# GpSimd takes the tables of the state-space branch, with new task tables for both first layers

## The reference

```python
lam_bar = jnp.exp(lam * dt)
b_bar = ((lam_bar - 1.0) / lam)[..., None] * b_c
bu = jnp.einsum("blgh,gph->blgp", uf.astype(jnp.complex64), b_bar)
_, states = lax.associative_scan(combine, (a_elems, bu), axis=1)
y = jnp.einsum("blgp,ghp->blgh", states, c_c).real
```

## Time and profile before

| what | value |
|---|---|
| median of three runs | 2157.72 us |
| the profiled execution | 2156.08 us, span 2154.3 us |
| TensorE busy | 2131.7 us, 99% of the span |
| VectorE busy | 1640.0 us, 76% |
| ScalarE busy | 1212.4 us, 56% |
| GpSimd busy | 56.4 us, 3% |
| granted TensorE clock | 0.999 of full speed |

### The profile page before, as it was taken

One profiled execution on the slowest core, in us unless ns is written; L12 is line 12 of the kernel. 1 busy time (PEld: TensorE's weight loads), 2 busy tenths in 40 slices (PEclk: granted clock), 3 DMA queues, 4 the chain that ended last, 5 costly groups with the idle time before them and its releaser, 6 DMA issues.

```text
span 2154.3 us, 47945 instructions
## 1 busy us (share of the span) xinstructions
PE 2131.7 (99%) x18740; PEld 2074.0 (96%) x18740; DVE 1640.0 (76%) x2626; ACT 1212.4 (56%) x1823; POOL 56.4 (3%) x54
## 2 busy tenths in 40 slices
PE   9999999999999999999999999999999999999998
PEld 8999999999999999899999999999899999999998
DVE  8997877987778766778947877766678947877764
ACT  6656544556656445446658845445446658845443
POOL 0000000000000000000002200000000002200000
PEclk9999999999999999999999999999999999999999
DMA  7444655644456556554544466556554544465553
GB/s 250 157 136 150 201 190 185 198 156 148 138 167 216 186 194 208 169 167 147 176 158 148 148 202 208 185 188 211 174 166 148 173 160 147 148 199 189 185 189 127
DMA packets 102976, 376.54 MB, mean 175 GB/s; under 512 B 11680, under 2 KB 11808, under 8 KB 102304
## 3 DMA queue, kind: packets, MB, share of 16 engines
q1 hardware_dynamic: 101664, 368.66, 52.7%
q10 hardware_dynamic: 1152, 5.58, 0.7%
HBM read 373.14 MB, written 1.05 MB: 174 GB/s over the span
## 4 chain that ended last, share of the span: by engine, by line
PE 90%; DVE 6%; ACT 2%; issue 1%; DMA 0%; DVEq 0%; ACTq 0%
PE acc L772 25%; PE acc L774 24%; PE acc L773 24%; DVE w_lo L1806 2%; PE acc L891 1%; PE acc L893 1%; PE acc L892 1%; PE acc L836 1%; PE acc L838 1%; PE acc L837 1%; ACT w_hi L1325 1%; PE mid L1128 1%; PE mid L1227 1%; DVE pr L2565 0%; PE mid L959 0%
## 5 line engine op out<-in xcount | busy, mean ns | idle before, releaser
L1806 DVE TENSOR_TENSOR w_lo<-w_raw,w_hi 128x1024 fp32r<-128x1024 f32 x694 | 847.8, 1226 | 321.5 <-ACT w_hi L1325 313.3
L1325 ACT CAST w_hi<-w_raw 128x1024 fp32r<-128x1024 f32 x694 | 723.8, 1046 | 541.2 <-PE acc L774 476.6
L772 PE MATMUL acc<-h_hi,w_hi 128*128 128x256 f32 x2096 | 600.1, 286 | 0.1
L773 PE MATMUL acc<-h_lo,w_hi 128*128 128x256 f32 x2096 | 589.3, 281 | 0.0
L774 PE MATMUL acc<-h_hi,w_lo 128*128 128x256 f32 x2096 | 586.2, 280 | 0.0
L772 PE MATMUL acc<-g_hi,w_hi 128*128 128x256 f32 x1456 | 412.6, 283 | 0.8 <-DVE w_lo L1806 0.7
L773 PE MATMUL acc<-g_lo,w_hi 128*128 128x256 f32 x1456 | 407.9, 280 | 0.0
L774 PE MATMUL acc<-g_hi,w_lo 128*128 128x256 f32 x1456 | 407.6, 280 | 0.0
L772 PEld LDWEIGHTS acc<-h_hi,w_hi 128*128 128x128 f32 x2096 | 394.0, 188 | 6.3 <-issue 5.0
L774 PEld LDWEIGHTS acc<-h_hi,w_lo 128*128 128x128 f32 x2096 | 396.1, 189 | 0.0
L773 PEld LDWEIGHTS acc<-h_lo,w_hi 128*128 128x128 f32 x2096 | 395.5, 189 | 0.5
(11 more groups left out here) (443 smaller groups left out, 3454.6 us busy)
## 6 DMA issues: line engine op xcount, KB each, us to landing
w_raw<-weights_d SPq DMA_DIRECT2D x695, 512.0 KB, 3.6
p<-p_d ACTq DMA_DIRECT2D x3, 1080.0 KB, 8.5
rdec<-decay_d ACTq DMA_DIRECT2D x2, 768.0 KB, 7.6
p<-p_d SPq DMA_DIRECT2D x1, 1024.0 KB, 10.8
out_d<-work SPq DMA_DIRECT2D x4, 256.0 KB, 2.3
x_all<-x_d SPq DMA_DIRECT2D x1, 516.0 KB, 4.4
w_raw<-weights_d SPq DMA_DIRECT2D x2, 256.0 KB, 5.8
x_all<-x_d SPq DMA_DIRECT2D x1, 512.0 KB, 6.2
```

Source lines behind the costliest of these rows:

```text
L772: mm(dst, wh, hi[:, k, :], start=first and j == 0, stop=False)
L773: mm(dst, wh, lo[:, k, :], start=False, stop=False)
L1325: nc.scalar.copy(w_hi[:, slot, :], w_raw[:, slot, :]).then_inc(hi_done, 1)
L1806: tt(w_lo[:, slot, :], w_raw[:, slot, :], w_hi[:, slot, :].bitcast(F32), SUB).then_inc(lo_v, 1)
```

## The change

Powers of B (`power 1..3`), clearing of `lag`, the six doublings of the first of the two layers, and `out_power 1..3` of both layers go from VectorE to GpSimd, which works through them in its own program order: powers, clearing, doublings (first layer only), output powers. GpSimd's powers wait for the parameters, for `fac` (new semaphore `v_fac`) and for the last slab that reads the memory under `tm`; `out_power 1` waits for `v_x`. `lag` moves to the memory of B's and C's parameters, so that it may be cleared before the lag products are made; it is three quarters as large. Both tables of tasks are new. In the feed-forward nothing moves. The doublings of the second of the two layers stay on VectorE.

```diff
+            def power(at, p):
+                i = STEP - 1 - p
...
+                times(by_re, b, l_re, ALU.mult)
+                times(by_im, b, l_im, ALU.mult).then_inc(p_step, 1)
+                pool.wait_ge(p_step, mine.next())
+                times(bs[0][:, :, i, :], by_re[:, 0, :, :], by_im[:, 1, :, :], ALU.subtract)
+                times(bs[1][:, :, i, :], by_re[:, 1, :, :], by_im[:, 0, :, :], ALU.add).then_inc(p_power, 1)
+                pool.wait_ge(p_power, at.n * 3 + p)
+            def powers(at):
+                if at.n == 0:
+                    pool.wait_ge(params, 16)
+                pool.wait_ge(v_fac, at.n + 1)
+                wait_used(pool, at, raw_end(at.n) - 1)
+            def lag_zero(at):
+                pool.wait_ge(a_power, at.n * 2 + 2)
+                pool.wait_ge(v_prep, at.n * 3 + 3)
+                nc.gpsimd.memset(lag[:, :, :, :], 0.0).then_inc(p_lag, 1)
+            def double(at, k):
...
+                times(new, old, cos_n, ALU.mult)
+                times(t, old, sin_n, ALU.mult).then_inc(p_step, 1)
+                pool.wait_ge(p_step, mine.next())
+                times(new[:, 0, :, :], new[:, 0, :, :], t[:, 1, :, :], ALU.subtract)
+                times(new[:, 1, :, :], new[:, 1, :, :], t[:, 0, :, :], ALU.add).then_inc(p_turn, 1)
+            def out_power(at, j):
...
+                if j == 1:
+                    pool.wait_ge(v_x, at.n + 1)
+                times(by_re, cab[:, :, :, :], l_re, ALU.mult)
+                times(by_im, cab[:, :, :, :], l_im, ALU.mult).then_inc(p_step, 1)
+            for n in range(DEPTH):
+                at = Layer(False, n)
+                powers(at)
+                lag_zero(at)
+                if n == 0:
+                    for k in range(6):
+                        double(at, k)
+                for j in range(1, STEP):
+                    out_power(at, j)
-                    pe.wait_ge(v_power, at.n * 3 + 3)
+                    pe.wait_ge(p_power, at.n * 3 + 3)
-                pe.wait_ge(v_ce, at.n * 3 + 3)
+                pe.wait_ge(p_ce, at.n * 3 + 3)
-                nc.vector.reciprocal(tiny[:, 17, :], tiny[:, 16, :])
+                nc.vector.reciprocal(tiny[:, 17, :], tiny[:, 16, :]).then_inc(v_fac, 1)
+                if at.n == 0 and j == 0:
+                    dve.wait_ge(p_turn, 6)
```

More of the change, by code:

```diff
@@ L127 @@
     {
[L128 to L133, removed]
-        12: (("out_table",),),
[L135 to L149, removed]
@@ L168 @@
-        50: (("pv", 4), ("pv", 5), ("pt", 6), ("pv_copy", 2), ("pt_copy", 6), ("pt", 7), ("pt_copy", 7), ("pv", 6),
-            ("pv", 7), ("pv_copy", 3), ("pv_lo", 3)),
+        3: (("mean",), ("roots",)),
+        4: (("rope", 0), ("rope", 1)),
+        5: (("h", 0), ("h", 1), ("h", 2), ("h", 3), ("lows",)),
+        6: (("scaled",),),
+        7: (("rope_mul", 0),),
+        9: (("prep_d",), ("rope", 2)),
+        11: (("power", 0),),
+        12: (("out_table",),),
+        15: (("rope_mul", 1), ("rope", 3)),
@@ new lines @@
+        16: (("spread", 0),),
+        19: (("rope_mul", 2), ("rope", 4), ("spread", 1)),
+        20: (("spread", 2),),
+        21: (("vt",), ("vt_copy",)),
+        22: (("rope_mul", 3), ("rope_mul", 4), ("tr", 0)),
+        23: (("tr_copy", 0),),
+        24: (("spread", 3), ("tr", 1), ("tr_copy", 1)),
+        26: (("tr", 2), ("tr", 3), ("tr_copy", 2), ("tr", 4), ("tr_copy", 3), ("tr", 5), ("tr_copy", 4),
+            ("tr_copy", 5), ("tr", 6), ("tr", 7)),
+        27: (("lag_copy", 0), ("lag_copy", 1), ("tr_copy", 6), ("tr_copy", 7), ("lag",)),
@@ new lines @@
+        29: (("lag_copy", 2),),
+        30: (("bu", 0), ("bu", 1), ("bu", 2), ("bu", 3)),
+        31: (("rot", 0), ("rot", 1), ("rot", 2), ("rot", 3)),
+        32: (("scores", 0), ("mask", 0), ("scan",)),
+        33: (("scores", 1), ("scores", 2)),
+        34: (("scores", 3),),
+        35: (("turn",), ("mask", 1)),
+        39: (("scores", 4), ("scores", 5), ("mask", 2), ("mask", 3), ("mask", 4), ("mask", 5)),
+        40: (("scores", 6), ("scores", 7), ("mask", 6), ("mask", 7)),
+        42: (("maxima",), ("softmax",), ("normalize",)),
@@ L170 @@
+        51: (("pv_lo", 3), ("pv", 6), ("pv", 7), ("pv_copy", 3)),
     },
@@ L172 @@
         1: (("mean",), ("roots",)),
[L173 to L190, removed]
-        27: (("scores", 0), ("scores", 1)),
@@ L192 @@
[L192 to L201, removed]
@@ new lines @@
+        14: (("vt",), ("vt_copy",)),
+        15: (("tr", 0), ("tr", 1), ("tr_copy", 0), ("tr", 2)),
+        16: (("tr_copy", 1), ("tr", 3), ("tr", 4), ("tr_copy", 2)),
+        17: (("tr_copy", 3), ("tr_copy", 4)),
+        18: (("tr", 5), ("tr_copy", 5), ("tr", 6), ("tr", 7)),
+        19: (("tr_copy", 6), ("tr_copy", 7)),
+        20: (("lag",), ("spread", 2), ("spread", 3)),
+        21: (("lag_copy", 0), ("lag_copy", 1), ("lag_copy", 2)),
+        23: (("bu", 0), ("bu", 1), ("rot", 0), ("bu", 2), ("rot", 1), ("bu", 3), ("rot", 2)),
@@ new lines @@
+        25: (("rot", 3),),
+        26: (("scan",),),
+        27: (("scores", 0), ("scores", 1)),
+        30: (("turn",),),
+        31: (("scores", 2), ("mask", 0)),
+        32: (("mask", 1), ("mask", 2)),
+        34: (("scores", 3), ("mask", 3), ("scores", 4), ("mask", 4)),
+        35: (("scores", 5), ("scores", 6), ("mask", 5), ("mask", 6)),
+        37: (("scores", 7), ("mask", 7), ("maxima",)),
+        39: (("softmax",),),
+        40: (("normalize",),),
+        42: (("cx",), ("ssm_y",)),
@@ L712, in squares_sum, with __init__, next @@
                 nc.gpsimd.tensor_tensor(zq[:, :], sqz[:, 0, :], sqz[:, 1, :], ALU.add).then_inc(p_zsum, 1)
+            class Products:
+                def __init__(self):
+                    self.n = 0
+                def next(self):
+                    self.n += 1
+                    return self.n
+            mine = Products()
+            times = nc.gpsimd.tensor_tensor
+            def power(at, p):
+                i = STEP - 1 - p
+                l_re, l_im = (fac[:, 2 * (p - 1) + part, :].unsqueeze(1).unsqueeze(3).to_broadcast([P, 2, PAIRS, PC])
+                              for part in range(2))
+                lo, hi = P1["b_re"][0], P1["b_im"][1]
+                b = p1[:, lo:hi].rearrange("p (r a c) -> p r a c", r=2, a=PAIRS)
+                by_re, by_im = (tm[:, k, :].rearrange("p (r a c) -> p r a c", r=2, a=PAIRS) for k in range(2))
+                times(by_re, b, l_re, ALU.mult)
[4 more added lines that the diff above has]
+                pool.wait_ge(p_power, at.n * 3 + p)
@@ new lines, in powers @@
+            def powers(at):
[3 more added lines that the diff above has]
+                wait_used(pool, at, raw_end(at.n) - 1)
+                for p in range(1, STEP):
+                    power(at, p)
+            def lag_zero(at):
[3 more added lines that the diff above has]
+            def double(at, k):
+                n = 1 << k
+                old, new = turn[:, :, :, 0:n], turn[:, :, :, n:2 * n]
+                cos_n, sin_n = (turn[:, part, :, n - 1:n].unsqueeze(1).to_broadcast([P, 2, PAIRS, n]) for part in range(2))
+                t = ptmp[:, :, 0:PAIRS * n].rearrange("p r (a c) -> p r a c", a=PAIRS)
+                times(new, old, cos_n, ALU.mult)
[3 more added lines that the diff above has]
+                times(new[:, 1, :, :], new[:, 1, :, :], t[:, 0, :, :], ALU.add).then_inc(p_turn, 1)
+                pool.wait_ge(p_turn, k + 1)
@@ new lines, in out_power @@
+            def out_power(at, j):
+                l_re, l_im = (fac[:, 2 * (j - 1) + part, :].unsqueeze(1).unsqueeze(3).to_broadcast([P, 2, PAIRS, PC])
+                              for part in range(2))
+                by_re, by_im = (tm[:, k, :].rearrange("p (r a c) -> p r a c", r=2, a=PAIRS) for k in range(2))
+                if j == 1:
+                    pool.wait_ge(v_x, at.n + 1)
+                times(by_re, cab[:, :, :, :], l_re, ALU.mult)
+                times(by_im, cab[:, :, :, :], l_im, ALU.mult).then_inc(p_step, 1)
+                pool.wait_ge(p_step, mine.next())
+                times(ce[0][:, :, j - 1, :], by_re[:, 0, :, :], by_im[:, 1, :, :], ALU.add)
+                times(ce[1][:, :, j - 1, :], by_re[:, 1, :, :], by_im[:, 0, :, :], ALU.subtract).then_inc(p_ce, 1)
+                pool.wait_ge(p_ce, at.n * 3 + j)
@@ L2098, in double @@
                 dve.wait_ge(dve_step, own.next())
[L2100 to L2132, removed]
             def scaled_tables(own):
```

68 lines of the change are left out of this document (35 added, 33 removed), and 4 rows, old and new, of the table ORDER1.

## The result

The changed kernel takes 2190.53 us (median of 4 runs, 2190.17 to 2190.97), beside 2157.83 us for the kernel before in the same comparison: a ratio of 1.0155, with an interval of [1.0142, 1.0168]. It is slower by 33 us. The profiled execution has a span of 2188.4 us, 34.1 more than before.

What follows compares the result with a forecast made beforehand. TensorE was taken as saturated, with VectorE's work covered by the ring of slabs. Terms 15.6 + 8.0 + 5 + 3 - 1.6 = 30 us on 2156.1 gave 2186, median 2188; range 2173 to 2206, chance 0.63.

Steps and rivals of the forecast that it cites:

- The mechanism: A VectorE instruction with both inputs in SBUF and a GpSimd one take turns, each waiting for the other's current one.
- the 7.7 us of waits: TensorE's five waits in the two changed layers before the change, taken as the most that lighter VectorE work could return.
- Steps 1 and 2: Output powers on GpSimd, first and second layer: ready late for `cx`, TensorE standing 15.6 and 8.0 us.
- sign of being wrong: GpSimd's output powers ready before slabs 45 and 42 end, or `w_lo` unchanged at 1.22 us.
- step 4: VectorE falling behind while GpSimd makes the powers of B: TensorE loses 5 us in the first layer, 3 in the second.
- Step 3: Powers of B on GpSimd: ready between 67 and 82 us, and 466 and 481; late by at most 4 us.
- The reserve: Lead of slab splits over their use, said to grow to some 6 us and subtracted from VectorE's lag.
- The count: VectorE's work during the powers of B, in microseconds: first layer 14 us behind, second layer 9, before subtracting 6.
- Step 5: The rest: clearing free, doublings covered by little, other table moves at no cost, `bt` wait perhaps gone: -1.6 us.
- The 1.2 us wait for `bt`: A TensorE wait in the kernel before, which the forecast said may go.
- The sum: All terms together: 30 us added to the profiled execution's 2156.1 us, giving 2186, or 2188 for the median.

Runs made afterwards that it cites:

- e1_two: Kernel before, VectorE's work untouched, GpSimd given twelve extra two-input products in each first layer, output unread: 2190.65 us, 1.0159.
- e1_fill: Kernel before, VectorE's work untouched, GpSimd given extra fills, which read no SBUF, in each first layer: 2156.32 us, 0.9998.
- e6_pieces: Changed kernel with each GpSimd product cut into four instructions of a quarter of the columns: 2191.44 us, 1.0164.
- e4_out: Kernel before with only the output powers moved to GpSimd, in both layers: 2168.19 us, 1.0059.
- e5_powers: Kernel before with only the powers of B moved to GpSimd, in both layers: 2183.10 us, 1.0127.
- e3_tables: Changed kernel, all moves in it, with the old order of tasks, moved tasks struck out: 2202.15 us, 1.0210.
- e2_fills: Changed kernel with each GpSimd product and sum replaced by a fill of the same output: 2154.21 us, 0.9992.

## Why the prediction was right in sum and wrong in its parts

**The mechanism** holds: GpSimd reading SBUF and VectorE with two inputs in SBUF run one after the other, each for a whole instruction. The earlier trace rows showed it in one place, and e1_two, e1_fill and e6_pieces show it from three sides. The Trainium skill's rule of an exclusive lock that is held for a whole instruction ("SBUF — State Buffer", the section on how the engine and DMA sides are separate) agrees with these rows, down to pieces of 0.6 us. Strict alternation is not always what follows: at 468.9 us (above) GpSimd's product takes 3.70 us, and three further products of VectorE (468.93 to 470.82) come ahead of it. The earlier trace rows was read a little short: the 7.7 us of waits leave out 1.8 us of smaller ones in the same two layers (L1035, L976, L1011), which touches no term of the sum.

**Steps 1 and 2, 15.6 and 8.0 us of waiting for `ce`, measured 0.** What the prediction had named as its sign of being wrong came: the output powers were ready before slab 45 and slab 42 of their layers ended (181.8 against 187.5, 603.8 against 607.3), and no wait of 8 to 16 us stands at `cx`. Three terms were off. GpSimd's 128x1024 was taken at 2.59 us and is 1.92 undisturbed, outside the bounds of 2.4 to 2.6: scaling the plain 128x256 and 128x512 rows up to this form was too dear. The turns lost were twelve at 1.22 and 3.7 more; the sets took 25.7 and 28.0 us instead of 39.2, and undisturbed they are 3 x (2 x 1.92 + 2 x 1.26) = 19.1, so 6.6 and 8.9 us were lost. And TensorE was not at `cx` at 161.6 (the rows give 161.7) but at 187.5, since step 4 had made it late, while `v_x` came at 155.9 instead of 138.0. `e4_out`, where step 4 hardly acts, has the wait: 4.9 us in the first layer, 0 in the second.

**Step 3, hidden or late by at most 4 us, was right for GpSimd itself.** The powers were ready at 68.0 us (forecast 67 to 82) and at 495.4 (466 to 481, with the 25.2 us by which that layer begins late 491 to 506), and TensorE never waited for them. What this step called hidden is what VectorE paid for in step 4: `e5_powers`, 28 us.

**Step 4, VectorE keeping up, 5 + 3 us, is the step that was mis-sized.** It is nearly the whole loss: 15.6 us by slab 20 and 17.4 by slab 31 in the first layer, 9.5 more in the second, and 7.4 under the scores, for which step 4 had no term at all. What went wrong in it:
- The reserve. I took 6 us; from the end of a split to the first matmul of its slab the trace of before has 2.6 to 4.9 us for slabs 12 to 16.
- The count. I counted VectorE's work by its microseconds. Under turn-taking a held instruction pays the rest of GpSimd's current one, whatever its own length: the chain of products of 16 columns just behind the reciprocal, 0.17 us each, lost 3.2 us in two of them, before any split. Six splits that belonged between 44 and 70 us were not made there.
- The clock. The lower granted clock behind each stand of TensorE is 8 us in all. TensorE's longest wait before is 2.2 us, and the sum had no term for it.
- The collision under the scores: a mask that came 4.0 us late behind four held splits, and its slab at the lower clock. Steps 1 and 2 charged the turns of that stretch to GpSimd alone and nothing to VectorE.

**Step 5** was right that the doublings are in time (made by 94.5 us, no wait for them) and gave their turns no price on VectorE, where `e3_tables` loses 4.9 us. It called the new tables neutral; with GpSimd reading they save 11.6 us, with fills and a relieved VectorE together 2 at most. The 1.2 us wait for `bt` did not go, it fell to 0.6.

**The sum** came out at 30 us where the profile has 34.1, because steps 1 and 2 had 23.6 us too much and step 4 some 26 too little. The two errors are of different causes, so their meeting was chance: the direction and the mechanism were foreseen, the size was luck.

## What to carry to other kernels

Before moving elementwise work to GpSimd, ask whether it reads SBUF, and put the turns on both engines' accounts: the cost is the VectorE work that has to meet a date in that stretch, counted in instructions, dependent small ones above all, against the reserve that the trace shows from the end of such work to its use. Work that only writes moved here at no cost that could be measured. Look also at which engine gets there first: a short wait or a changed order decides which of the two is held (`h_lo`, 2.5 or 8.1 us). Price each stand of a saturated TensorE above its own length, and when a total agrees with the forecast, look for the wait that the forecast named before believing it.

## What was not expected of the hardware

- Two VectorE products of 16 columns took 1.78 us each beside GpSimd products of 1.92 and 1.94 us.
- A TENSOR_SCALAR with one input tensor and one operand by pointer (128x256, 0.35 us as a rule) took 1.55 us and ended 0.15 us behind the GpSimd product of 51.94 us; in the earlier trace rows I had set the limit at two tensors in SBUF. The Trainium skill ("SBUF — State Buffer", the same section) names two-port modes of VectorE beside two inputs; the trace doesn't show the mode, so which of them this was stays open. The same instruction is held beside a fill too, which reads nothing: in `e2_fills` it takes 0.55 us and ends 0.14 us behind the fill of 47.67.

```profile
48.22 0.55 DVE L2331 TENSOR_SCALAR ccx<-zpad,p 128x256 f32<-128x256 f32 x1
```

- Apart from that one, no VectorE instruction of the kernel before that overlaps a fill in `e1_fill` or `e2_fills` is longer than there by 0.1 us (fills of 128x2048 take 1.82 us). Copies with one input (1.31 to 1.39 us in the mean for 128x1024) do hold VectorE; they cost a quarter of what the products cost for half of their busy time.
- GpSimd's product of 128x1024 with a broadcast input takes 1.92 us undisturbed, of 128x512 1.26, of 128x256 in a piece 0.61.
- The granted clock fell to 0.5 to 0.7 in windows of 4 to 5 us around idle stretches of TensorE of 2.4 to 5.4 us, and the y matmuls behind a stand of 4.9 us had 0.50 for 4.5 us.
